# Indexer key and weight columns in one weight slot, an empty slot before the output projection, and the vector engine's indexer splits ahead of the memory's

## What is computed

```python
h = rms_norm(x, mix_norm[l])
z = h @ w_in[l]
aq, ak, av, iq, ik, iw, pu, mq = jnp.split(z, IN_OFFSETS, axis=-1)
# widths: aq, ak, av 512 each; iq 256; ik 64; iw 4; pu 256; mq 256
# indexer: four heads iq, one key ik, four weights iw per token
score = sum_h iw[t, h] * relu(iq[t, h] . ik[s]);  each query keeps its top 128 keys
y_attn = attention(aq, ak, av) over the kept keys, 8 heads of 64
y_pool = multiscale_pool(pu);  y_mem = attention(mq, memory keys, memory values), 4 heads
x = x + jnp.concatenate([y_attn, y_pool, y_mem], axis=-1) @ w_out[l]
```

## Time and profile before

| | |
|---|---|
| median of 3 executions | 1983.04 us (1982.92 to 2177.24) |
| profiled execution, first to last instruction (span) | 1981.4 us |
| median less span | 1.6 us |
| PE busy | 1948.7 us, 98% |
| ACT busy | 1086.5 us, 55% |
| DVE busy | 617.1 us, 31% |
| POOL busy | 350.7 us, 18% |
| transfers | 354.54 MB, mean 179 GB/s |

### The profile page before, as it was taken

One profiled execution on the slowest core, in us unless ns is written; L12 is line 12 of the kernel. 1 busy time (PEld: TensorE's weight loads), 2 busy tenths in 40 slices (PEclk: granted clock), 3 DMA queues, 4 the chain that ended last, 5 costly groups with the idle time before them and its releaser, 6 DMA issues.

```text
span 1981.4 us, 27709 instructions
## 1 busy us (share of the span) xinstructions
PE 1948.7 (98%) x9256; PEld 1571.9 (79%) x9256; DVE 617.1 (31%) x1180; ACT 1086.5 (55%) x1393; POOL 350.7 (18%) x404
## 2 busy tenths in 40 slices
PE   6999999999999999999999999999999999999999
PEld 4888888886768888888878888888767688888887
DVE  3222200367662322220052222004676532222101
ACT  6655543563584655553375565336546666565432
POOL 1111111111431111111111111111116111111111
PEclk9999999999999999999999999999999999999999
DMA  7988888887336888888878888888762379888886
GB/s 217 218 188 192 195 190 194 190 192 176 83 87 144 195 188 190 193 194 194 195 170 200 189 186 199 196 195 200 185 155 54 87 170 206 194 197 189 195 195 180
DMA packets 97799, 354.54 MB, mean 179 GB/s; under 512 B 11000, under 2 KB 11256, under 8 KB 97472
## 3 DMA queue, kind: packets, MB, share of 16 engines
q0 software_dynamic: 47232, 171.99, 48.7%
q1 hardware_dynamic: 49824, 178.84, 27.5%
q10 hardware_dynamic: 672, 2.80, 0.4%
HBM read 179.52 MB, written 2.10 MB: 92 GB/s over the span
## 4 chain that ended last, share of the span: by engine, by line
PE 97%; DMA 1%; ACT 1%; issue 1%; DVE 0%; SPq 0%; DVEq 0%; ACTq 0%; POOLq 0%
PE bank L453 95%; PE bank L806 2%; DMA w_lo<-raw 1%; DMA x<-x_t 0%; ACT w_lo L920 0%; ACT prob L1066 0%; DVE pt L336 0%; ACT a_hi L1082 0%; ACT t L1066 0%; DVE t L1323 0%; DVE x L1150 0%; DVE z L1277 0%; ACT pt L1059 0%; ACT mv L1046 0%; DVE yt L1341 0%
## 5 line engine op out<-in xcount | busy, mean ns | idle before, releaser
L919 ACT ACTIVATE w_hi<-raw 128x1024 fp32r<-128x1024 f32 x329 | 349.0, 1061 | 645.5 <-PE bank L453 630.8
L453 PE MATMUL bank<-h_hi,w_hi 128*128 128x512 f32 x1664 | 654.6, 393 | 15.9 <-ACT h_hi L891 13.9
L453 PE MATMUL bank<-h_hi,w_lo 128*128 128x512 f32 x1664 | 649.5, 390 | 5.6 <-DMA w_lo<-raw 5.6
L453 PE MATMUL bank<-h_lo,w_hi 128*128 128x512 f32 x1664 | 632.9, 389 | 0.0
L385 POOL DMA_DIRECT2D w_lo<-raw x328 | 283.5, 866 | 1589.6 <-ACT w_lo L920 1549.7
L453 PEld LDWEIGHTS bank<-h_hi,w_hi 128*128 128x128 f32 x1664 | 313.3, 188 | 97.5 <-ACT h_hi L891 15.3
L453 PEld LDWEIGHTS bank<-h_hi,w_lo 128*128 128x128 f32 x1664 | 313.3, 188 | 71.3 <-DMA w_lo<-raw 6.1
L453 PEld LDWEIGHTS bank<-h_lo,w_hi 128*128 128x128 f32 x1664 | 312.4, 188 | 65.5 <-issue 1.2
L920 ACT ACTIVATE w_lo<-raw 128x1024 fp32r<-128x1024 f32 x329 | 343.5, 1044 | 0.0
L453 PE MATMUL bank<-a_hi,w_hi 128*128 (+2 forms) x864 | 334.1, 387 | 0.0
L453 PE MATMUL bank<-a_lo,w_hi 128*128 (+2 forms) x864 | 332.8, 385 | 0.0
(11 more groups left out here) (138 smaller groups left out, 1273.9 us busy)
## 6 DMA issues: line engine op xcount, KB each, us to landing
raw<-weights SPq DMA_DIRECT2D x332, 512.0 KB, 4.6
w_lo<-raw POOLq DMA_DIRECT2D x328, 512.0 KB, 5.7
x<-x_t SPq DMA_DIRECT2D x4, 512.0 KB, 7.3
mem<-mem_t ACTq DMA_DIRECT2D x2, 1024.0 KB, 7.1
out_t<-x SPq DMA_DIRECT2D x8, 256.0 KB, 2.1
const<-consts SPq DMA_DIRECT2D x1, 505.5 KB, 10.1
spread_in<-spreads ACTq DMA_DIRECT2D x2, 216.0 KB
wpool<-pool_w ACTq DMA_DIRECT2D x2, 128.0 KB, 7.0
```

What stands on the lines that cost most here:

```text
L453: return nc.tensor.matmul(out_, lhsT, rhs, start=start, stop=stop, skip_group_check=True)
L919: nc.scalar.activation(w_hi[:, s], raw[:, s], ACT.Copy).then_inc(w_hi_done, 1)
```

## The change

The four iw columns move into the ik slot, behind the 64 ik columns (which now stand there once), and the iw slot goes. So that the stream keeps 32 slots in the mixing block, a slot of zeros named "empty" is put ahead of out. The slots of iq and ik keep their numbers, av to mv move one down (mv is 87 and 88), empty is 89, out stays 90 to 97. PE does nothing for the empty slot; the last product of mv counts both slots as used.

```diff
-MIX_SLOTS = (("iq", 2), ("ik", 1), ("iw", 1), ("av", 4), ("aq", 4), ("ak", 4), ("mq", 2), ("pu", 2),
-             ("mk", 2), ("mv", 2), ("out", 8))
+MIX_SLOTS = (("iq", 2), ("ik", 1), ("av", 4), ("aq", 4), ("ak", 4), ("mq", 2), ("pu", 2),
+             ("mk", 2), ("mv", 2), ("empty", 1), ("out", 8))
...
-OUT_ROUND_UNITS = (9, 11, 21, 23)
+OUT_ROUND_UNITS = (7, 9, 11, 21, 23)
...
-            ahead = MIX_BASE["out"]
+            ahead = MIX_BASE["empty"]
...
                 project(l, at("ik"), bank[2][:, :], h_hi, h_lo)
-                project(l, at("iw"), bank[3][:, :], h_hi, h_lo)
-
                 pe.wait_ge(rms_ready, l * 3 + 2)
...
-                            last.then_inc(slot_done, 1)
+
+                            last.then_inc(slot_done, 2 if s == 1 else 1)
...
-                round_ahead(l, MIX_BASE["ik"])
-                nc.scalar.activation(sq[:, 0:DC * MEM], mem[:, :], ACT.Square).then_inc(msq_ready, 1)
                 for j in range(3):
                     act.wait_ge(proj_ready, l * 17 + (j + 1))
                     nc.scalar.activation(chunk(idx_hi, j), chunk(idx, j), ACT.Copy)\
                         .then_inc(idx_hi_ready, 1)
-                round_ahead(l, MIX_BASE["iw"])
+                round_ahead(l, MIX_BASE["ik"])
+                nc.scalar.activation(sq[:, 0:DC * MEM], mem[:, :], ACT.Square).then_inc(msq_ready, 1)
...
-                        round_ahead(l, MIX_BASE["out"] - RING + OUT_ROUND_UNITS.index(n))
+                        round_ahead(l, MIX_BASE["empty"] - RING + OUT_ROUND_UNITS.index(n))
...
+                for j in range(2):
+                    evacuate(j, MIX_BASE["iq"] + j, chunk(idx, j), bank[j][:, :], r[:, :])
+
+
+                dve.wait_ge(slot_done, l * SLOTS + (RING + MIX_BASE["ik"] + 1))
+                for half in range(2):
+                    p = slice(half * HD, (half + 1) * HD)
+                    last = V.tensor_tensor(out=chunk(idx, 2)[p, :], in0=bank[2][0:HD, :],
+                                           in1=r[0:HD, :], op=ALU.mult)
+                last.then_inc(proj_ready, 1)
+                V.tensor_tensor(out=iw[0:IDX_HEADS, :], in0=bank[2][HD:HD + IDX_HEADS, :],
+                                in1=r[HD:HD + IDX_HEADS, :], op=ALU.mult).then_inc(proj_ready, 1)
```

More of the change, by code:

```diff
@@ L1186, in evacuate @@
                     V.tensor_tensor(out=out_, in0=in_, in1=rr, op=ALU.mult).then_inc(proj_ready, 1)
-                for j in range(3):
-                    evacuate(j, MIX_BASE["iq"] + j, chunk(idx, j), bank[j][:, :], r[:, :])
+                for j in range(2):
[8 more added lines that the diff above has]
+                                in1=r[HD:HD + IDX_HEADS, :], op=ALU.mult).then_inc(proj_ready, 1)
+                for j in range(3):
+                    dve.wait_ge(idx_hi_ready, l * 3 + (j + 1))
+                    V.tensor_tensor(out=chunk(idx_lo, j), in0=chunk(idx, j),
+                                    in1=chunk(idx_hi, j).bitcast(f32),
+                                    op=ALU.subtract).then_inc(idx_lo_ready, 1)
+                dve.wait_ge(cols_done, l + 1)
+                V.tensor_copy(cols[:, :], bank[3][:, 0:TT + 4 * TT]).then_inc(cols_ready, 1)
+                dve.wait_ge(cols_ready, l + 1)
                 dve.wait_ge(msq_ready, l + 1)
@@ L1196, in mix @@
                                 op=ALU.add).then_inc(mssq_ready, 1)
[L1197 to L1213, removed]
                 n = 0
@@ L1227, in mix @@
                         wait_apart(dve, acc_score, l * 12 + n)
+                dve.wait_ge(m_hi_ready, (l + 1) * DC)
+                for j in range(DC):
+                    s = slice(j * MEM, (j + 1) * MEM)
+                    last = V.scalar_tensor_tensor(out=m_lo[:, s], in0=mem[:, s],
+                                                  scalar=par[:, ds(l * PARAMS + (G_MEM + j), 1)],
+                                                  in1=m_hi[:, s].bitcast(f32), op0=ALU.mult,
+                                                  op1=ALU.subtract)
+                last.then_inc(m_lo_ready, 1)
                 def take_largest(before):
@@ L1436, in _weight_stream @@
     kv = a["w_mem_kv"][l]
-    iw = np.concatenate([iw, np.zeros((D, P - 4), iw.dtype)], 1)
+    ik = np.concatenate([ik, iw, np.zeros((D, P - ik.shape[1] - iw.shape[1]), iw.dtype)], 1)
     parts = ffn(a["ffn1_gate"][l], a["ffn1_up"][l], a["ffn1_down"][l])
-    parts += [_by_output(iq, 2), _by_output(np.concatenate([ik, ik], 1), 1), _by_output(iw, 1),
+    parts += [_by_output(iq, 2), _by_output(ik, 1),
               by_tokens(av, 2), _by_output(aq, 4), _by_output(ak, 4), _by_output(mq, 2),
               _by_output(pu, 2), _by_output(kv[:, :256], 2), by_tokens(kv[:, 256:], 4),
-              a["w_out"][l].reshape(DC, P, SLOT)[OUT_ORDER]]
+              np.zeros((1, P, SLOT), w.dtype), a["w_out"][l].reshape(DC, P, SLOT)[OUT_ORDER]]
     parts += ffn(a["ffn2_gate"][l], a["ffn2_up"][l], a["ffn2_down"][l])
```

## The result

The changed kernel took **1995.86 us** (median of 6, 1993.67 to 1996.20) against 1982.90 us before (median of 6), a ratio of **1.0065, 95% interval [1.0055, 1.0075]**. That is 13 us slower, under the 2% that count as a difference here, but outside the range of the prediction, 1979 to 1989. One of the six executions of the kernel before took 2177.24 us, far above its other five (1979.34 to 1983.04), and does not enter the ratio. The profiled execution took 1996.2 us, 1994.0 of them span.

A forecast was written before the change was run, and what follows sets the result against it. PE, 97% of the chain, was taken to bound the kernel. 1981.4 - 10.9 (projection) + 9.3 (wait) + 3.4 (clock) = 1983.2 us span, plus 1.6 between span and median: 1984.8 us; range 1979 to 1989.

The forecast's parts named there:

- The removed projection: Start of the mixing block: 24 matmuls gone take 5.44 us off PE's path per layer, 10.9 us for two.
- the av projection: First projection behind ik: weights and bank 4 are ready before 399.25, so PE does not wait.
- `dots(2)`: PE's dot products behind the first scores: scores come 1.0 us late, but this stays hidden by 0.9 us.
- The reordering serves it without adding to it: DVE and ACT, mixing block: the new order supports the removed projection's 10.9 us and gains nothing more.
- The mechanism of the loss: Attention loop: slot 89's late transfer delays slot 93, ACT's copy and PE by 4.65 us a layer, 9.3 for two.
- the size of the load of slot 93: SP's load behind the pooling: takes 5.8 us from its issue at 563.57, landing at 569.4.
- The rival on contention: Attention loop: slot 93's load slowed to 7.4 us by POOL's transfers, 1991.0 us; chance 0.11, including times above 1988.
- The clock: PE behind the new wait: half clock over 3 to 4 us of work costs 1.7 us a layer, 3.4 for two.
- the one on `rt`: PE's later wait in the attention loop, 1.38 us before 569.70, was to stay as it was.
- the 1.38 us wait at 569: PE, attention loop, before the change: clock stayed at 2.4 GHz, taken as trace and rule differing on such waits.
- the empty slot's rounding after unit 7: ACT, attention loop: 1.9 us more, alone costing PE 0 to 1.2 us a layer, but swallowed by the longer wait.

The follow-up runs named there:

- the kernel with the load alone: The changed kernel, but POOL, after slot 89's transfer, waits until slot 93 is loaded before sending slot 90 and the rest; 1984.05 us, ratio 1.0005.
- the order alone: The kernel before, its iw projection kept, with only the indexer's splits moved ahead of the memory's on DVE and ACT; 1981.97 us, ratio 0.9998.
- the projection back: The changed kernel with slot 89 rounded and transferred before the attention loop, plus 24 unused matmuls per layer on the ik slot; 1982.49 us, ratio 0.9998.

## Why the prediction was wrong

**The removed projection: right.** 5.44 us for each layer at the transposes, to the hundredth. PE did not wait at the av projection, nor at `dots(2)`. DVE kept to its forecast:

```profile
405.00 1.90 DVE L1201 TENSOR_TENSOR idx_lo<-idx,idx_hi 128x512 fp32r<-128x512 f32 x3
412.33 0.18 DVE L1205 COPY cols<-bank 128x20 f32<-128x20 f32 x1 [5.44 <-PE bank L453]
412.55 1.95 DVE L1209 TENSOR_TENSOR sq<-sq 128x1024 f32<-128x1024 f32 x2
...
414.88 0.48 DVE L1222 SCALAR_TENSOR_TENSOR score<-t,cols,const 128x256 f32<-128x256 f32 x1
```

`idx_lo` was done at 406.9 (forecast 407), the first score began at 414.88 (414.7). "The reordering serves it without adding to it" held as well: 2.7 us would be lost without it.

**The mechanism of the loss: right.** Slot 89 behind the pooling, slot 93 behind it, ACT behind that, PE behind ACT, in both layers, with the clock at 0.50 behind the wait.

**The step that failed: the size of the load of slot 93**, "I take the 5.8 of the load itself, since it is issued at the same place with the same neighbours". The place was the same within 0.1 us (4.86 behind POOL's first transfer). The neighbours were not. Before, POOL had issued three transfers behind the pooling by 563.57 (two from 558.78 on, one at 563.37), not the two that the prediction counted, and the first had landed: two were open, one of them for only 0.2 us. Now it had issued four by the load of the first layer, three of them open; in the second layer two were open and the third came 0.84 us later. The load took 10.3 and 7.6 us. With POOL's and SP's issue and ACT's request as measured, the wait is 4.86 + 10.3 - 6.08 = 9.1 us and 4.84 + 7.6 - 6.95 = 5.5 us; the rows on ACT say 9.13 and 5.54. For PE it came to 15.1 us where 9.3 stood. The rival on contention had the right mechanism with the wrong end: it took the slowest of the four loads, 7.4 us, though it said itself that one transfer more would be about than in those rows. The range, too, allowed no load slower than that.

**The clock: the kind right, the size not.** Forecast were 3.4 us for both layers. Take from the 23.4 us that came back the 15.1 us of the new wait: 8.3 us are left. 4.3 of them are three falls outside the attention loops, behind `cols` in both layers and at the border (+1.48, +1.45, +1.33 in the table), of which the prediction had none. The other 4.0 lie in the loops, where waits on DVE grew by some 2.3 (`pt` by 1.7, `negmax` by 0.6) and the one on `rt`, which the prediction had staying "as it did", shrank by 1.9, from 2.8 to 0.9; so nearly all of it is work at half clock. That this comes near the forecast of 3.4 is luck. Behind the two new waits half clock held 5.6 and 6.8 us of work, not the 3 to 4 us of the prediction, which costs 6.2 us; but the fall ahead of them, at 530 in the first layer, was 3.4 us long in this profile instead of 6.8, and that gave 1.7 back, which leaves 4.5 us by this count and 3.6 by the balance. The prediction also took the 1.38 us wait at 569 for a difference between trace and rule. The example in that section of the Trainium skill ("TensorE: Matmul & The Clock Gate", section "HAM oscillation — how this bites in real kernels") has waits longer than the bursts between them, so a short wait that keeps the clock does not speak against it.

Of the empty slot's rounding after unit 7 the prediction said that it is swallowed by the longer wait; no run here takes it alone out of the changed kernel, so its own price stays open.

## What to carry to other kernels

An unused slot in a ring is not free: it passes through every hand but the last, and what counts is which other load waits for its passing, so put its passage where those hands are idle. When a transfer moves into a burst of others, its duration has to be taken from a row with the same neighbours, counted one by one with the engine that issues them and with the time that each has been out, and if there is no such row the bound must lie beyond the slowest one seen. And a distance between two engines that is read from a trace can hold a fall of the clock; when the clock moves, the distance does.

## What the hardware showed unexpectedly

- A 512 KB load from memory took 3.2 us with none of POOL's 512 KB transfers open at its issue, 5.8 with two, 7.6 with two and a third 0.84 us later, and 10.3 with three. In the last case SP's queue had 23.8% of the engines' time, POOL's 79.5%. The number alone does not set it. Over all ten traces and both layers, SP's first load behind the pooling took 4.4 to 6.0 us with two open of which the later had been out for 0.2 us (seven loads), 7.5 to 8.8 us with two that had both been out for over 1 us (nine), and 9.0 to 10.3 us with three open (four; two of these are the load that follows slot 93 in the kernel with the load alone).
- About the same wait lowered the clock in one kernel and not in the other. At the border of the layers PE waits for a low part. Before the change:

```profile
1005.43 0.50 PE L453 MATMUL bank<-h_hi,w_hi 128*128 128x512 f32 x1 [1.99 <-DMA w_lo<-raw]
1005.77 0.40 PE L453 MATMUL bank<-h_hi,w_lo 128*128 128x512 f32 x1
```

and in the changed kernel:

```profile
1011.89 0.79 PE L453 MATMUL bank<-h_hi,w_hi 128*128 128x512 f32 x1 [1.88 <-DMA w_lo<-raw]
1012.48 0.63 PE L453 MATMUL bank<-h_hi,w_lo 128*128 128x512 f32 x1
```

  The shorter wait was followed by 3.4 us at half clock, the longer by none. One profile of each kernel shows a fall at the border in all seven kernels without the projection of iw and in none of the three with it (the kernel before, the order alone, the projection back); why is not known. The fall behind `cols` came in neither layer of the kernel before and of the one with the projection back, in both layers of the changed kernel, and in one or both of the others. Runs of one kernel differ in this too: that with the load alone took 1980.51 us at a mean clock of 0.993 and 1985.31 us at 0.991. What decides a single fall stays open. The Trainium skill ("TensorE: Matmul & The Clock Gate", section "HAM oscillation — how this bites in real kernels") has bursts with waits between them pay for the slow clock again and again. The waits of 9.31 and 5.79 us, in which the clock fell at 564 and 1554, agree with it, and the pair at the border lies outside its example, whose waits are longer than the bursts: for short ones this case shows that the length of the wait alone does not tell.
